# The gate block's product cut into parts between the rounds of a recurrence, and a new order of the projection, in a two-block layer on one core

## The reference

```python
h = rms_norm(x, norm_mix_g[l])
u = h @ w_in[l]
y_ssd = ssd_mixer(u[..., :SSD_IN], ...)
y_rwkv = rwkv7_mixer(u[..., SSD_IN:], ...)
x = x + jnp.concatenate([y_ssd, y_rwkv], axis=-1) @ w_out[l]
...
# ssd_mixer: the gate z (1024 columns), xbc (1536), dt (16)
z, xbc, dt = jnp.split(u, [SSD_WIDTH, SSD_WIDTH + SSD_CONV_DIM], axis=-1)
xbc = jax.nn.silu(causal_depthwise_conv(xbc, conv_w, conv_b))
...
y = y_diag + y_off + xs * d_skip
y = y.reshape(bsz, seq, SSD_WIDTH) * jax.nn.silu(z)      # z is wanted only here
...
# rwkv7_mixer: r, k, v of 1024 columns each, and low-rank (LoRA) columns
uf = uf + (u_prev - uf) * mu
kk = heads(k * k_k); kk = kk / jnp.maximum(norm(kk), 1e-12)
k = k * (1.0 + (iclr - 1.0) * k_a)
def step(state, inp):                                    # over 256 positions
    r_t, w_t, k_t, v_t, kk_t, a_t = inp
    sa = jnp.einsum('bhij,bhj->bhi', state, -kk_t)
    state = state * w_t + sa * (kk_t * a_t) + v_t * k_t
    return state, jnp.einsum('bhij,bhj->bhi', state, r_t)
```

## Time and profile before

| | us |
|---|---|
| three runs | 2844.91, 2844.86, 2843.03 |
| median | 2844.86 |
| span of the profiled execution | 2846.5 |
| TensorE busy in it | 2803.9 (99%) |
| DVE busy | 1735.5 (61%) |
| ACT busy | 1315.8 (46%) |
| GpSimd busy | 43.6 (2%) |
| mean granted TensorE clock | 0.997 |
| Z's halves | 255.9 to 302.4 |
| recurrence with SSD | 302.4 to 448.3 |
| additions with `w_out` from | 451.8 |

### The profile page before, as it was taken

How to read it: one execution, slowest core, us unless ns; L and a number is a source line. 1 busy time by engine, 2 the same in 40 slices (tenths; PEclk the granted TensorE clock), 3 DMA queues, 4 the chain that set the end, 5 groups by cost and what they waited for, 6 DMA issues and landing times.

```text
span 2846.5 us, 40996 instructions
## 1 busy us (share of the span) xinstructions
PE 2803.9 (99%) x17275; PEld 2398.9 (84%) x17275; DVE 1735.5 (61%) x2053; ACT 1315.8 (46%) x1672; POOL 43.6 (2%) x71
## 2 busy tenths in 40 slices
PE   8999899999999999999999999999999999999998
PEld 7888788788888888888888888888888888888886
DVE  5688666654445555555555666655666756665665
...
GB/s 232 177 193 176 77 47 150 186 182 192 179 135 183 186 192 192 191 193 183 197 190 189 189 180 190 178 169 174 161 180 198 185 195 190 187 198 192 190 181 132
DMA packets 392420, 504.60 MB, mean 177 GB/s; under 512 B 11360, under 2 KB 285293, under 8 KB 391213
## 3 DMA queue, kind: packets, MB, share of 16 engines
...
...
## 4 chain that ended last, share of the span: by engine, by line
PE 95%; DVE 3%; ACT 1%; issue 1%; DMA 0%; ACTq 0%; SPq 0%; DVEq 0%
PE PS L639 37%; PE PS L644 33%; PE PS L648 17%; PE PS L864 3%; PE PS L676 1%; DVE wlo L1889 1%; PE PS L996 0%; PE PS L1012 0%; PE PS L804 0%; PE PS L784 0%; PE PS L1045 0%; DMA slab<-in_x 0%; ACT whi L1287 0%; PE PS L819 0%; PE PS L1036 0%
## 5 line engine op out<-in xcount | busy, mean ns | idle before, releaser
L1889 DVE TENSOR_TENSOR wlo<-raw,whi 128x1024 fp32r<-128x1024 f32 x922 | 1127.0, 1228 | 791.1 <-ACT whi L1287 787.5
L1287 ACT ACTIVATE whi<-raw 128x1024 fp32r<-128x1024 f32 x922 | 970.3, 1057 | 963.3 <-PE PS L648 497.9
L644 PE MATMUL PS<-XX,whi 128*128 128x512 f32 (+1 forms) x3856 | 1216.8, 397 | 0.0
L648 PEld LDWEIGHTS PS<-XX,wlo 128*128 128x128 f32 (+1 forms) x3856 | 724.5, 188 | 171.3
L648 PE MATMUL PS<-XX,wlo 128*128 128x256 f32 (+1 forms) x3856 | 759.7, 278 | 0.0
L639 PE MATMUL PS<-whi,act 128*128 128x512 f32 x2240 | 602.1, 391 | 0.0
L644 PEld LDWEIGHTS PS<-XX,whi 128*128 128x128 f32 (+1 forms) x3856 | 589.3, 189 | 2.8 <-DVE wlo L1889 0.6
L639 PEld LDWEIGHTS PS<-whi,act 128*128 128x128 f32 x2240 | 418.0, 188 | 85.3
L639 PE MATMUL PS<-wlo,act 128*128 128x512 f32 x1120 | 344.9, 389 | 0.0
L639 PE MATMUL PS<-whi,XX 128*128 128x512 f32 x1024 | 280.8, 396 | 6.5 <-DVE wlo L1889 5.1
L639 PEld LDWEIGHTS PS<-wlo,act 128*128 128x128 f32 x1120 | 210.2, 188 | 44.0
...
## 6 DMA issues: line engine op xcount, KB each, us to landing
raw<-in_ffn_w SPq DMA_DIRECT2D x128, 1024.0 KB, 5.5
...
```

Source lines behind the costliest of these rows:

```text
L644: T.matmul(ps[0:wd, f, :], whi[:, o:o + wd], b.x[:, kk, :], start=first, stop=False, skip_group_check=True)
L648: mm = T.matmul(ps[0:wd, f, 0:SEQ], wlo[:, o:o + wd], b.x[:, kk, 0:SEQ], start=False, stop=last, skip_group_check=True)
L1287: S.activation(k.whi[:, h % 4, 0:b.size], k.raw[:, t % 4, u * b.size:(u + 1) * b.size], ACT.Copy).then_inc(k.w_hi, 1)
L1889: V.tensor_tensor(k.wlo[:, h % 4, 0:b.size], k.raw[:, h // 2 % 4, u * b.size:(u + 1) * b.size], k.whi[:, h % 4, 0:b.size].bitcast(F32), AL ...
```

## The change

Four things. **Z in parts:** Z's 16 halves are still last in the stream, but they are no longer a stretch of their own. `TensorStream.parts` stops in the middle of a half, and in each of the first 26 rounds of the recurrence TensorE multiplies one or two of the 32 parts between a chunk's round and an SSD step (`gate_halves` gives how far Z is after round n: 3 halves after round 0, 16 after round 25). Both Z blocks use the same banks 0 and 1; banks 2 and 3 are the SSD's. A list `SSD_AT` says which of 44 rounds has an SSD step. **Order:** r, k, v come key first (columns 2, 3, 0, 1, 4, 5), the LoRA steps end one block earlier, the preparation ends two halves before the end of XBC, and the SSD's transposes lie in the recurrence. **Scratch off the input operand:** the recurrence's buffers, `chunk_own` and places in the slab, no longer overlap `XX`, which Z's parts read until round 25; the SSD has two decay buffers and not three, its tiles go in another order, and x is loaded again only after the recurrence. **Work moved from DVE:** the mixing's first term, the first convolution tap, `k * k_k` and the factor with `k_a` are made on ACT with scales per feature; r_k is multiplied into the constant `sel_rk` once. Besides, `dynamic_dma_scratch_size=1024` is given when the program is built.

```diff
-SSD_STEPS = 33
+ROUNDS = 44
+
+SSD_AT = frozenset([*range(3, 8), *range(9, 17), *range(22, 44)])
...
-                b = Block(kind, j, w, k0, kt, col, mode, x, there, part, len(self.blocks), self.tiles, more)
+                number = len(self.blocks)
+                parity = self.blocks[-1].parity if kind == "tok" and "alone" in more else number % 2
+                b = Block(kind, j, w, k0, kt, col, mode, x, there, part, number, self.tiles, parity,
+                          len([o for o in self.blocks if o.parity == parity]), more)
...
-        for j in range(6):
-            put("rkv", j, w, 2576 + 512 * j, "feat", rows=True)
+        for j, cols in enumerate((2, 3, 0, 1, 4, 5)):
+            put("rkv", j, w, 2576 + 512 * cols, "feat", rows=True, cols=cols)
...
         for j in range(2):
-            put("tok", j, w, 512 * j, "tok", dst=self.Z, func=ACT.Silu, row=0)
+            put("tok", j, w, 512 * j, "tok", dst=self.Z, func=ACT.Silu, row=0, **({"alone": True} if j else {}))
...
 class TensorStream(Stream):
+    part = None
+
     def half(self, h):
+        run(self.parts(h))
+
+    def parts_to(self, n):
+
+        while 2 * self.at + (self.part is not None) < n:
+            if self.part is None:
+                self.part = self.parts(self.at)
+                next(self.part)
+            else:
+                run(self.part)
+                self.part, self.made, self.at = None, self.at + 1, self.at + 1
+
+    def parts(self, h):
         k = self.k
         T, (b, q, u) = k.nc.tensor, k.halves[h]
         ps = k.PS[:, 2 * b.parity:2 * b.parity + 2, :]
-        if h == b.first and b.number >= 2:
+        if h == b.first and b.turn:
             T.wait_ge(*k.free(b))
         T.wait_ge(k.w_lo, h + 1)
...
+            if a == b.kpt // 4 - 1:
+                yield
         mm.then_inc(k.w_used, 1)
 
...
 def prepared(s, steps):
 
-    s.spread(itertools.islice(steps, EARLY_AT), EARLY_AT, s.k.half_at("xbc", 2) + 5)
-    s.spread(steps, PREP_STEPS - EARLY_AT, s.k.half_at("tok", 1))
-
-
-def split_between(s, steps):
-
-    s.fence = len(s.k.halves)
-    for n in range(LEAD):
-        s.prepare(n + 1)
-        next(steps)
-    run(steps)
+    s.spread(itertools.islice(steps, PREP_FIRST), PREP_FIRST, s.k.half_at("xbc", 0) + 2)
+    s.spread(steps, PREP_STEPS - PREP_FIRST, s.k.half_at("xbc", 2) - 2)
+
+
+def gate_halves(n):
+
+    return min(16, 3 + 13 * n / 25)
+
+
+def beside_gates(s, chunk_steps, ssd_steps):
+
+    gates = s.k.half_at("xbc", 2)
+    for n in range(ROUNDS):
+        next(chunk_steps)
+        if n in SSD_AT:
+            next(ssd_steps)
+        s.to(gates + int(gate_halves(n)))
+        if n == ROUNDS - LEAD - 1:
+            s.flush()
+            s.fence = len(s.k.halves)
+        if n >= ROUNDS - LEAD:
+            s.prepare(n + 1 - ROUNDS + LEAD)
+    run(chunk_steps)
+    run(ssd_steps)
 
 
...
+    s.spread(lora_pe(k), LORA_STEPS, k.half_at("rkv", 2))
+    s.to(k.half_at("rkv", 2) + 2)
+    prepared(s, prep_pe(k))
+    s.to(k.half_at("xbc", 2))
     T.wait_ge(*k.rp.DVE("end"))
     T.wait_ge(*k.ri.DVE("z"))
-    T.wait_ge(*k.sd.DVE("ncs"))
-
-    chunk_steps, ssd_steps = chunks(chunk_pe, k), ssd_pe(k)
-    next(chunk_steps)
-    next(ssd_steps)
-    steps = side_by_side(ssd_steps, chunk_steps)
-    advance(steps, SSD_STEPS - 1)
+
+    chunk_steps, ssd_steps, gates = chunks(chunk_pe, k), ssd_pe(k), 2 * k.half_at("xbc", 2)
+    for n in range(ROUNDS):
+        next(chunk_steps)
+        s.parts_to(gates + int(2 * gate_halves(n)))
+        if n in SSD_AT:
+            next(ssd_steps)
+    run(chunk_steps)
+    run(ssd_steps)
     T.wait_ge(*k.sd.DVE("xl7"))
-    run(steps)
     s.spread(halves_of(post_pe, k), POST_STEPS, k.half_at("add", 2))
...
             d = b.arg["dst"][:, :, 512 * j:512 * j + 512]
             if b.number == k.blocks_of("tok")[0].number:
-                S.wait_ge(*k.rp.DVE("kn"))
+                S.wait_ge(*k.sd.PE("st"))
...
                 S.activation(d, d, b.arg["func"]).then_inc(k.evacuated[b.parity], 1)
+        if b.kind == "rkv" and b.s:
+            yield
+            k.wait_both(S, b)
+            S.wait_ge(k.rest_made, 1)
+            for f in range(4):
+                f0 = 4 * b.arg["cols"] + f
+                at = RP + f0
...
 def prep_act(k):
     S, rp = k.nc.scalar, k.rp
-    S.wait_ge(*rp.DVE("kr"))
+    S.wait_ge(*k.mix.DVE("m", 1))
+    for f in range(RP):
+        ins = S.activation(k.KK[:, f, :], k.RKV[:, 8 + f, :], ACT.Copy, scale=k.col["rwkv_k_k"][:, f:f + 1])
...
         if q == 1:
             yg = k.y[:, c, g * 512:g * 512 + 512]
             V.wait_ge(*sd.PE(f"y{n}"))
             V.wait_ge(*sd.POOL(f"y{c}"))
-            for b in k.blocks_of("tok")[0:2]:
-                V.wait_ge(*k.out_of_psum(b))
-            k.dve(V.tensor_tensor(yg, yg, PS[:, 1, :], ALU.add))
...
             t = b.tile + q
             if t == 4:
                 rest_sync(k)
-            if t == behind_chunks:
-                decays_sync(k)
+            if t == first + 5:
+                decays_sync(k, 0, 2)
+            if t == first + 8:
+                decays_sync(k, 2, 8)
```

More of the change, by code:

```diff
@@ L763, in ssd_pe @@
     yield
[L764 to L770 removed]
+    T.wait_ge(*sd.ACT("st"))
     for n in range(8):
[L773 to L774 removed]
+        c, g, q = ssd_group(n)
         if q == 0:
@@ L2750, in sync_program @@
     x_sync(k, Y, 0)
[L2752 removed]
+    first = k.half_at("xbc", 2) // 2
     for b in k.blocks:
```

261 lines of the change are left out of this document (136 added, 125 removed).

## The result

Four runs of the kernel after: 2865.81, 2867.99, 2866.02 and 2870.37 us, median **2867.0 us**, against 2844.7 us before; the ratio is 1.0079, 95% interval 1.0068 to 1.0091. It is slower by 22 us, outside the forecast range of 2833 to 2858. It was the fastest of the four after, and the profiled one before was slower than its median: some 4 of the 22 us are in no ledger.

The account below looks back on a forecast made before the run. TensorE bounds the kernel, busy 2803.9 of 2846.5 us. 2846.5 - 19.8 (old idle and clock) + 16.1 (new waits) + 2.9 (switches) + 3.3 (clock) = 2849.0, less 1.6 for the median: 2847.4 us, range 2833 to 2858.

Parts of the forecast that it names:

- half 88: First half of Z's second block: TensorE waits 2.6 us for Z's first block to leave PSUM (1.6 to 4.0).
- y4: SSD tile after chunk 1: a wait of 3.9 us (2.4 to 4.6), four output operations standing ahead of the decays.
- z1 of chunk 2: Round 30, after Z is used up: a wait of 2.4 us behind the four output operations (1.3 to 3.3).
- The wait ahead of the post stage: Existing wait before the post stage: stays at 1.1 us, as the change touches no cause of it.
- p3: Products of the third power in chunk 0: a wait of 1.3 us behind whi, wlo and DVE's own operation (0 to 1.3).
- y0: SSD tile in round 9: a wait of 1.2 us behind wlo, chunk additions, decays and product on DVE (0 to 1.2).
- GpSimd's skip product: At y0, would collide with a DVE operation: left out of the sum, +1.1 us (to 2.1) put in the range.
- The rest costs nothing: Key first, LoRA and other moved steps, work moved to ACT, later x load: no added time.
- the price of half 78: End of the preparation: TensorE waits 1.6 us for DVE's queue up to that half's wlo (0 to 4).
- The switches: Z's parts entered behind other work in the recurrence: 29 times 0.1 us, 2.9 us in all (0 to 2.9).
- The clock: TensorE in the recurrence: one fall to the lower clock, at y4, costing 3.3 us (bounds none and three).
- rival B: Slower: the clock falls at all three long waits, half 88, y4 and z1, 3.3 us each; 2854.0 us, chance 0.20.

Follow-up runs that it names:

- run four: The kernel after, with the SSD's four-operation outputs of the second 128 positions one step earlier on DVE; 2858.9 us.
- nine: The kernel before, with DVE's product of an SSD tile ahead of the next tile's decays, from the second tile on; 2841.4 us, ratio 0.9989.
- run one: The kernel before, with the LoRA steps spread to the end of the second r, k, v block instead of the third, on all three engines; 2850.8 us, ratio 1.0018.
- run two: The kernel after, with TensorE alone one half further in the stream when its LoRA steps begin; 2865.5 us.

## Why the prediction was wrong

**Right.** That idle time in the recurrence would be left at about its old amount, by new waits in place of the old. Three of the eight waits came as worked out: half 88 with 2.43 us (forecast 2.6), y4 with 3.76 (3.9), z1 of chunk 2 with 2.46 (2.4). Their arithmetic, what stands on the engine ahead, start to start, less the products between, is confirmed by runs four and nine. The wait ahead of the post stage stayed at 1.08 (1.1). The one at p3, forecast at 1.3, did not come at all, for a reason that isn't shown. It is in part luck, then, that the idle time of this stretch, 17.5 us, came near the forecast 14.5: p3's 1.3 us make up for some of what y0 and chunk 3 took more. The table load behind Z's evacuation took 1.28 us again, and GpSimd's skip product held nobody up: it began at 318.38, 0.23 us behind DVE's L2238, which took 0.69 us, and DVE had nothing more to do until it was done; the range that I had set aside for it was not used.

**The step that failed first: "The rest costs nothing".** It covered the LoRA steps, and for them named no cover at all. They cost a wait of 2.94 us, which run one brings into the kernel before and run two takes out of after. The diff moves their end by one block; what counts is that TensorE's first of them comes a half earlier, with ACT's chain ahead of it no shorter. Another 1.42 us (155.84) came from the denser first steps of the preparation: DVE does four mixing operations, a reciprocal of 1.75 us and a wide product ahead of a `wlo`. No run changed that place alone, so this cause is read from the timeline and not tested.

**The second: the price of half 78,** 1.6 us, measured 4.06 with 1.6 us of clock. I counted DVE's queue from an evacuation that I took to be in time. DVE was late there already, because ACT was, as I read it from the timeline; no run moves ACT's work. ACT's timeline of after, ahead of it (L1639 and L1641 are the preparation's wide exponentials, L1351 the evacuation):

```profile
233.13 1.92 ACT L1639 ACTIVATE slab<-slab 128x2048 f32<-128x2048 f32 x1 [0.49 <-DVE slab L2331]
235.09 1.92 ACT L1641 ACTIVATE slab<-slab 128x2048 f32<-128x2048 f32 x1
236.91 1.99 ACT L1315 ACTIVATE whi<-raw 128x1024 fp32r<-128x1024 f32 x2
238.80 0.58 ACT L1351 ACTIVATE slab<-PS 128x512 f32<-128x512 f32 x1
```

```profile
237.98 2.36 DVE L1942 TENSOR_TENSOR wlo<-raw,whi 128x1024 fp32r<-128x1024 f32 x2 [2.61 <-ACT whi L1315]
240.26 0.69 DVE L1957 TENSOR_TENSOR slab<-PS,slab 128x512 f32<-128x512 f32 x1
...
243.88 1.67 DVE L2069 SCALAR_TENSOR_TENSOR slab<-slab,param_cols 128x256 f32<-128x256 f32 x4 [0.89 <-ACT slab L1373]
```

DVE stands 2.61 us for `whi`, then has the evacuation still to do, and stands 0.89 us again for L1373, the convolution tap that the change gave to ACT. TensorE begins half 72 at 238.4, so by the forecast the evacuation starts at 239.0; it starts at 240.26. From there to the end of `wlo` 78 at 259.10 it is 18.8 us and not 17.8. The two make 2.3 of the 2.5 us that were missing. The tail's exponentials, pulled forward, and an edit meant to relieve DVE made DVE wait for ACT.

**The third: terms that were too small.** The switches cost 5.6 us (4.3 by the other reading in run four) and not 2.9, since I had the way in (0.10) and not the way back. y0 waited 2.07 us and not 1.2: ACT's copy of the states, table load, exponential and `whi` stood ahead of DVE's `wlo`, and I had counted DVE alone. Chunk 3 waits 0.49, 1.09 and 1.04 us where before had none; no term stood for this. DVE's timeline of after has a `wlo` of `w_out` and an operation on the SSD's last output (L2272) ahead of each of these rounds' evacuations, and that of before has neither from 430 us to the end of chunk 3; no run tests it:

```profile
454.11 0.47 DVE L2272 SCALAR_TENSOR_TENSOR XX<-PS,param_cols,XX 128x256 fp32r<-128x256 f32 x1
455.01 1.23 DVE L1942 TENSOR_TENSOR wlo<-raw,whi 128x1024 fp32r<-128x1024 f32 x1 [0.42 <-ACT whi L1315]
456.15 0.75 DVE L2382 TENSOR_TENSOR slab<-PS,slab 128x256 f32<-128x256 f32 x2
```

The clock cost 5.3 to 6.1 us in this stretch, forecast 3.3, and 1.6 ahead of it: rival B's mechanism was at work, at the three places it named and in chunk 3, with falls of 1.4 to 1.7 us each and not 3.3. It had 0.20.

**The ledger** of the 18.1 us: ahead of Z 2.9 + 1.4 + 4.1 of waits, 1.6 of clock and 0.6 of small ones, 10.6; then idle time +0.9, switches +5.6, clock +1.6, 8.1; behind, 0.6 less. The forecast had 1.6 for the first and +0.9 for the second sum (-16.6 of removed waits and -3.2 of clock against 14.5 + 2.9 + 3.3).
